# Down weights of passes 6 to 28 in 4 MB transfers, and the activation turned by 64x64 products

## What is computed

```python
for e in range(N_EXPERTS):
    hid = x @ w_up[e] + b_up[e]                      # w_up[e]: 1024 x 2048 float32, 8 MB
    x_glu = jnp.minimum(hid[..., ::2], SWIGLU_LIMIT)
    x_lin = jnp.clip(hid[..., 1::2], -SWIGLU_LIMIT, SWIGLU_LIMIT)
    act = x_glu * jax.nn.sigmoid(SWIGLU_ALPHA * x_glu) * (x_lin + 1.0)
    out = out + gate_full[:, e:e + 1] * (act @ w_down[e] + b_down[e])   # w_down[e]: 1024 x 1024, 4 MB
```

## Time and profile before

| | us |
|---|---|
| median of 3 runs | 1103.95 (1103.44 to 1104.15) |
| the profiled execution, its own time | 1102.51 |
| its span in the trace | 1100.7 |
| TensorE busy | 1041.7 (95%) |
| VectorE busy, ScalarE busy | 253.7, 194.3 |
| mean rate of the DMA engines over the span | 389 GB/s |

### The profile page before, as it was taken

The page is one execution under the profiler, slowest core; times in us unless marked ns, Lnnn a source line. Parts: engine busy times, 40 slices in busy tenths (PEclk is TensorE's granted clock), DMA queues, the critical chain, the costliest instruction groups (busy, mean ns, idle before and its releaser), DMA issues.

```text
span 1100.7 us, 12751 instructions
## 1 busy us (share of the span) xinstructions
PE 1041.7 (95%) x5191; PEld 452.2 (41%) x5191; DVE 253.7 (23%) x660; ACT 194.3 (18%) x365; POOL 8.1 (1%) x25
## 2 busy tenths in 40 slices
PE   8989999999999999999999999989999999899985
PEld 8978665333333333333333333333333333333321
DVE  6796353211111111111111111011111111111113
ACT  5593221111111111111010111111111111110110
POOL 2000000000000000000000000000000000000000
PEclk9999999999999999999999999999999999999999
DMA  9724798999999999999999999999999999999993
GB/s 323 222 93 117 297 380 329 382 417 429 428 429 430 431 429 433 429 434 429 428 433 425 432 432 428 431 427 429 429 428 432 434 427 432 428 432 424 425 426 123
DMA packets 39168, 428.33 MB, mean 389 GB/s; under 512 B 4240, under 2 KB 17584, under 8 KB 20464
## 3 DMA queue, kind: packets, MB, share of 16 engines
q1 hardware_dynamic: 37584, 427.18, 93.0%
q10 hardware_dynamic: 1536, 0.43, 0.2%
HBM read 426.02 MB, written 1.05 MB: 388 GB/s over the span
## 4 chain that ended last, share of the span: by engine, by line
PE 53%; DMA 42%; DVE 4%; ACT 1%; issue 0%; DVEq 0%; SPq 0%; ACTq 0%
PE bank L1488 22%; DMA ring<-in_w_up_dram 19%; PE bank L1546 12%; DMA tail_mem<-in_w_up_dram 8%; DMA ring<-in_w_down_dram 6%; DMA wbuf<-in_w_up_dram 4%; DMA wbuf<-in_w_down_dram 4%; PE bank L1207 3%; PE bank L1260 3%; PE bank L1446 2%; PE bank L1224 2%; PE bank L1431 2%; PE bank L1439 1%; PE bank L1532 1%; PE bank L1499 1%; PE bank L1518 0%
## 5 line engine op out<-in xcount | busy, mean ns | idle before, releaser
L1488 PE MATMUL bank<-ring,wbuf 128*64 128x512 f32 x1248 | 285.5, 607 | 21.2 <-DMA ring<-in_w_up_dram 20.5
L1488 PEld LDWEIGHTS bank<-ring,wbuf 128*64 128x64 f32 x1248 | 90.5, 139 | 190.7 <-issue 156.7
L1546 PE MATMUL bank<-ring,wbuf 128*64 128x512 f32 x640 | 141.5, 593 | 3.8 <-DMA ring<-in_w_down_dram 3.3
L693 ACT ACTIVATE wbuf<-wbuf 128x256 f32<-128x256 f32 x64 | 26.7, 417 | 521.1 <-DVE wbuf L1128 521.1
L1128 DVE TENSOR_SCALAR wbuf<-bank 128x256 f32<-128x256 f32 x64 | 26.8, 419 | 352.0 <-PE bank L1488 352.0
L1488 PE MATMUL bank<-tail_mem,wbuf 128*64 128x512 f32 x416 | 96.7, 613 | 8.0 <-DMA tail_mem<-in_w_up_dram 8.0
L1488 PE MATMUL bank<-wbuf 128*64 128x512 f32 x384 | 87.7, 604 | 4.6 <-DMA wbuf<-in_w_up_dram 4.6
L1112 DVE TENSOR_SCALAR hT<-iota_s,hT 128x128 f32<-128x128 f32 x64 | 19.3, 343 | 290.7 <-PE bank L1518 289.6
L1546 PEld LDWEIGHTS bank<-ring,wbuf 128*64 128x64 f32 x640 | 45.5, 137 | 96.0 <-issue 87.1
L1446 PE MATMUL bank<-wbuf,putT 64*128 64x512 f32 x264 | 65.6, 615 | 0.7 <-ACT wbuf L698 0.7
L1431 PE MATMUL bank<-X,hT 128*64 128x512 f32 x256 | 60.5, 593 | 0.1
(11 more groups left out here) (242 smaller groups left out, 783.8 us busy)
## 6 DMA issues: line engine op xcount, KB each, us to landing
ring<-in_w_up_dram SPq DMA_DIRECT2D x29, 4096.0 KB, 41.5
ring<-in_w_down_dram SPq DMA_DIRECT2D x39, 2048.0 KB, 38.1
ring<-in_w_up_dram SPq DMA_DIRECT2D x20, 2048.0 KB, 14.7
wbuf<-in_w_up_dram SPq DMA_DIRECT2D x10, 4096.0 KB, 40.7
tail_mem<-in_w_up_dram SPq DMA_DIRECT2D x9, 4096.0 KB, 41.8
tail_mem<-in_w_down_dram SPq DMA_DIRECT2D x12, 2048.0 KB, 35.9
wbuf<-in_w_down_dram SPq DMA_DIRECT2D x12, 2048.0 KB, 39.6
tail_mem<-in_w_up_dram SPq DMA_DIRECT2D x8, 2048.0 KB, 18.9
```

Of the source, the lines that this page charges most:

```text
L693: a.activation(sig[:, w], glu[:, w], ACT.Sigmoid, scale=SIG_ALPHA).then_inc(s["sig_ready"], 1)
L1488: ins = mm(bank[n][c * SLOTS:(c + 1) * SLOTS, :], xT[:, k, :], wk[:, o:o + 512], start=(k == 0), stop=(k == KT - 1))
L1546: ins = mm(bank[2][c * SLOTS:(c + 1) * SLOTS, :], actT[:, at:at + SLOTS], wk[:, a * D + c * 512:a * D + (c + 1) * 512], start=(i == 0 and ...
```

## The change

The view of the down weights takes eight neighbouring rows of `w_down` to a partition instead of twice four rows from two halves, so that a partition's part of an expert's 4 MB is one run of 32768 bytes. Buffer i then holds rows 8 p + 4 i to 8 p + 4 i + 3 on partition p. `joined` takes in the down weights of passes 6 to 28; in the other passes the two buffers are loaded one by one, each with half of the run. Feature 8 p + i must now be on partition p of the turned activation. Every eighth column of `act_` gives 64 columns; partitions 0 to 63 of `act_` hold features 0 to 511 and keep their place, partitions 64 to 127 hold 512 to 1023 and keep theirs. So `act_turned` makes sixteen products of 64x64 with a part of the identity, in pairs on opposite quadrants of the array, after one `keep_warm` product into the same bank; and the index `at` in `down` follows.

```diff
-        dn_v = w_down[0].rearrange("e (i p a) n -> e i p (a n)", p=P, a=4)
+        dn_v = w_down[0].rearrange("e (p a) n -> e p (a n)", p=P)
...
         def joined(n):
             p, c = what(n)
-            return FIRST_DOUBLE <= p < FIXED and c < UPC
+            return FIRST_DOUBLE <= p < FIXED and (c < UPC or p < FIXED - 1)
...
             if c >= UPC:
-                return dn_v[p, c - UPC] if isinstance(p, int) else dn_v[bass.ds(p, 1), c - UPC].rearrange("o p n -> (o p) n")
+                w = slice((c - UPC) * CW, (c - UPC + 1) * CW)
+                return dn_v[p, :, w] if isinstance(p, int) else dn_v[bass.ds(p, 1), :, w].rearrange("o p n -> (o p) n")
...
         def load_two(sp, n):
             p, c = what(n)
-            sp.dma_start(buffer(n, 2), up_v[p, c // 2]).then_inc(chunk_in[n % BUFS], 16)
+            src = up_v[p, c // 2] if c < UPC else dn_v[p]
+            sp.dma_start(buffer(n, 2), src).then_inc(chunk_in[n % BUFS], 16)
...
             def act_turned(p):

                 pe.wait_ge(s["act_ready"], 2 * p + 2)
-                for i in range(4):
-                    ins = tr(bank[3][:, i * P:(i + 1) * P], act_[:, i::4], ident[:, :])
+                keep_warm(bank[3], 1)
+                for i in range(8):
+                    for c in range(2):
+                        r = slice(c * SLOTS, (c + 1) * SLOTS)
+                        ins = mm(bank[3][r, i * SLOTS:(i + 1) * SLOTS], act_[r, i::8], ident[r, r], start=True, stop=True)
                 ins.then_inc(s["actT_ps"], 1)
...
-                        at = a * P + i * SLOTS
+                        at = (i * 4 + a) * SLOTS
```

## The result

The changed kernel takes **1106.89 us** (median of 5 runs, 1106.75 to 1109.22) against 1103.44 of the kernel before measured beside it: ratio **1.0038, 95% interval 1.0025 to 1.0052**. It is slower by about 4 us. The prediction said 1105.2 with a range of 1102.4 to 1110.0, and gave "within 0.2%" the largest chance; the measured interval lies above 0.2%, on the side that had 0.34.

What follows compares the result with a forecast made beforehand. The DMA engines were taken as the bound from 240 us to the last landing, TensorE before and behind. Transfers -1.7, two early turnings +1.94, tail +0.97 make +1.2 us; on the median, 1105.2 us, range 1102.4 to 1110.0.

Steps and rivals of the forecast that it cites:

- the surplus: Extra TensorE time per act_turned, sixteen products and warming against four transposes: 0.97 us taken, between 0.48 and 2.47.
- the spare 2.62 us: From 240 us to the last landing, TensorE needs 26.62 us a pass, the DMA engines 29.24.
- the three exposed turnings: act_turned of passes 0 and 1, ahead of dry DMA engines (+1.94 us), and the last, in the tail (+0.97).
- The cover at the first joined load: Queue of issued transfers at the first 4 MB down load: 12.2 us, 8.8 with the late issue.
- The transfers: Down weights of passes 6 to 28 in 4 MB transfers: -1.7 us, ends at 0 and -3.
- Passes 2 to 29: 0: Longer turning under full DMA engines costs nothing while below the spare time and not eating the cover; good to 2.2 us.
- The joined waits: Down products wait for all 4 MB, up to 2.8 us, replacing the wait at up products; price 0.
- Rival (e): Longer waits before down products lower TensorE's clock; lag carried into the tail, at most 2 us: 1107, chance 0.05.
- rival (b): act_turned in passes 0, 1 and last: strided weights load one after another, surplus 2.47, +5.7 us, 1109.7; chance 0.17.
- (a): Rival in act_turned: the step costs nothing in quadrants, surplus 0.48, sum -0.3 us, 1103.7; chance 0.20.
- (c): Rival in the transfers: large packets gain more, -5 us, with a lower-end surplus, 1100.4; chance 0.08.
- (d): Rival in the transfers: the DMA rate stays, so no gain, +2.9 us, 1106.9; chance 0.08.

Runs made afterwards that it cites:

- first_two: Kernel before with the new row order, 64x64 products and warming product in passes 0 and 1 alone, all down weights in 2 MB transfers; ratio 1.0029.
- spare_7: Kernel before with seven warming products added ahead of act_turned in passes 2 to 29; ratio 1.0023.
- spare_20: Kernel before with twenty warming products added ahead of act_turned in passes 2 to 29; single run, 1166.46 us against 1106.26.
- late_only: Kernel before with the whole change (row order, 4 MB down transfers, 64x64 products) in passes 6 to 28 alone; ratio 1.0005.
- after: The changed kernel itself, against the kernel before; 1106.89 us, ratio 1.0038.
- turn_only: Changed kernel without its 4 MB down transfers: new row order and 64x64 products in all passes, down weights in 2 MB; ratio 1.0064 against the kernel before.

## Why the prediction came out as it did

**The bound, and where the surplus counts: right.** The pace of the DMA engines, the spare 2.62 us, and the three exposed turnings (passes 0, 1 and the last) are confirmed by the issues (+1.7, +3.4), by first_two, spare_7, spare_20 and late_only. The page's 98% and the chain's 85% for TensorE after the change are the trap here: late_only keeps 97% and 78% and loses nothing. The cover at the first joined load was close to its end, as worked out (8.8 - 4 x 1.74 = 1.8 us left): issued at 353.50 us, it lands after 13.7, where a 4 MB transfer into dry engines would take some 7.8 + 4.9 = 12.7.

```profile
ring<-in_w_down_dram SPq DMA_DIRECT2D x1, 4096.0 KB, 13.7
```

**The surplus: mis-sized.** This is the step that failed. I took 0.97 us and measured 1.74 (31.84 - 30.10 at the issues, 28.36 - 26.62 in the pace, 5.30 - 3.57 in the tail, all within 0.01). Of the 0.77 that are missing, 0.20 are the warming product (0.42 for 0.22; I priced it as one of a row of its kind, and it stands alone; whether that is why was not tried) and 0.57 the pieces: 64.4 ns for the 47 of "both quadrants load side by side". The two ends of the range, 31.6 and 94 ns, hold the value; the middle was chosen by an argument, not by a row, and a term that counts three times deserved the middle of its ends (1.5 us), not the lower third.

**That 1105.2 is only 1.7 us off is partly luck.** Between the profiled executions, which start alike, I expected +1.2 us and the spans have +4.4. Three times 0.77 are 2.3 of the 3.2 that are missing, and most of the rest is the term for code below. The forecast had added 1.44 us for the distance of the median from the profiled execution; in the changed kernel the median is the profiled execution within 0.02 us, and that hid part of the error.

**The transfers: -1.7 said, -1.8 measured between after and turn_only, which have the same code.** Right in size; the 428 GB/s that it was worked out from are rounded, which is some 0.4 us either way here, so that the two agree to 0.1 is luck. As a net number in the changed kernel it is -1.1 because of the next point.

**Code loading: not in the sum.** I gave no price to the 960 products and as many loads that the engine has to fetch. In the DMA stage about +1.0 us comes with them. "Passes 2 to 29: 0" holds for TensorE's time. It left out the loading of the instructions, which goes over the engines that are the bound.

**The joined waits: priced at 0, right.** They moved as described: none left before up products, 1.8 us in all before down products. Rival (e) did not show in the changed kernel, whose clock is 1.00 in the stage, where the longest wait at the down products is 0.8 us; it showed in spare_7. The point that rival (b) named, a surplus of 1.3, was passed, but not for its reason: the quadrants do overlap in part. (a) is excluded by the 64.4 ns, (c) and (d) by the table of shares.

Sum with the measured terms: 3 x 1.74 - 1.8 + 1.0 = +4.4 us, as the spans have it. Each of the last two is good to 0.5, and the agreement is closer than that: the first pair of traces has -1.1 for both together and 0.4 behind the last down products, which nothing here explains.

## What to carry to other kernels

Where a queue of transfers is the bound, an engine at 98% may still be free: price an added instruction by whether the queue is dry or full at its place, at the head and the tail of the stage above all, and check by putting the addition only into the covered part. Read strided operands of TensorE with a step of at most two floats, or have an idle engine write them in the order needed. And count code as time of the DMA engines: unrolled instructions share them with the weights (a packet of 16 KB set the last engine back by 1.1 to 1.4 us here), and a transfer ends with its slowest engine.

## What the runs showed of the hardware that I had not expected

- 8192 idle instructions on GpSimd, 64 loads of 8 KB, cost 28 us of 1104 in a kernel bound by DMA: one engine fell up to 34 us behind, some 0.6 us for a packet that took 0.31.
- The 16 shares of a transfer drift apart over the run, from 1 to 2 us to 7 to 9, in two groups of eight; the share of the last engine falls back by 1.1 to 1.4 us with every eighth load of TensorE's code. The DMA share of 1.00 in a window doesn't show that.
- 64x64 fp32 pieces on alternating quadrants: 33.8 ns without a step or with a step of two, 64.4 with four or eight; 111 with a step of eight on one quadrant.
- The clock of the first 20 us differs between executions of one kernel (granted 1.00, 0.91, 0.83), which moves what follows by 0, 1.6 or 2.8 us, and later spells near 165 and 205 us add to it: total times fall on levels (1101.9, 1103.6, 1105.4 for the kernel before), and differences below 2 us are read better inside traces than from medians.
